# A decoder layer on one core: the combining of the gate/up products moves from VectorE to GpSimd, and the gate/up weights come packed

## The reference

```python
h = rmsnorm(x, ffn_norm[l])
gate = jnp.einsum('bsd,df->bsf', h, w_gate[l])      # d = 2048, f = 5632
up = jnp.einsum('bsd,df->bsf', h, w_up[l])
x = x + jnp.einsum('bsf,fd->bsd', jax.nn.silu(gate) * up, w_down[l])
return rmsnorm(x, final_norm)
```

## Time and profile before

| | |
|---|---|
| median of three runs | 2033.67 us |
| the profiled execution: its time, and the span of its instructions | 2032.2 us, 2030.4 us |
| ScalarE busy | 1005.3 us (50%) |
| GpSimd busy | 142.7 us (7%) |
| gate/up stage | from about 656 us (first L1524) to about 1563 us |
| granted TensorE clock, mean | 0.999 |

### The profile page before, as it was taken

The page is one execution under the profiler, slowest core; times in us unless marked ns, Lnnn a source line. Parts: engine busy times, 40 slices in busy tenths (PEclk is TensorE's granted clock), DMA queues, the critical chain, the costliest instruction groups (busy, mean ns, idle before and its releaser), DMA issues.

```text
span 2030.4 us, 30889 instructions
## 1 busy us (share of the span) xinstructions
PE 2013.3 (99%) x10492; PEld 1720.2 (85%) x10492; DVE 1528.3 (75%) x2250; ACT 1005.3 (50%) x1874; POOL 142.7 (7%) x235
## 2 busy tenths in 40 slices
PE   9999999999999999999999999999999999999998
PEld 7888888887888988888888888888888888888886
DVE  5666666666766999898999999999998546546446
ACT  6455555554436654555555455554555323333333
POOL 0122222221100000000000000000000000000000
PEclk9999999999999999999999999999999999999999
DMA  8222222224234344444444444444447653544433
GB/s 295 83 75 72 77 72 73 73 72 153 76 99 155 116 139 131 132 138 125 139 137 132 138 137 136 127 141 133 131 138 243 241 179 99 177 154 120 140 96 133
DMA packets 263774, 265.32 MB, mean 131 GB/s; under 512 B 14080, under 2 KB 194560, under 8 KB 262656
## 3 DMA queue, kind: packets, MB, share of 16 engines
q1 hardware_dynamic: 249136, 224.97, 36.8%
q0 software_dynamic: 6336, 23.07, 2.9%
q10 hardware_dynamic: 8208, 15.98, 2.2%
HBM read 232.51 MB, written 31.46 MB: 130 GB/s over the span
## 4 chain that ended last, share of the span: by engine, by line
PE 75%; DVE 10%; issue 7%; ACT 4%; DMA 3%; SPq 1%; ACTq 0%; DVEq 0%; POOLq 0%; POOL 0%
PE bank L556 20%; PE bank L560 10%; PE bank L489 10%; PE bank L490 10%; PE bank L491 10%; PE bank L445 4%; PE bank L447 4%; PE bank L446 4%; DVE t_lo L1533 3%; DMA t_raw<-in_w_up 2%; ACT probs L848 1%; ACT w_hi L805 1%; PE bank L608 1%; DVE part L1542 1%; DVE w_lo L1250 1%
## 5 line engine op out<-in xcount | busy, mean ns | idle before, releaser
L556 PE MATMUL bank<-s_two,t_hi 128*128 128x512 f32 x2352 | 609.9, 392 | 2.7 <-ACT part L1070 1.3
L1250 DVE TENSOR_TENSOR w_lo<-raw,w_hi 128x512 fp32r<-128x512 f32 x364 | 253.2, 697 | 382.0 <-ACT w_hi L805 379.9
L1030 ACT ACTIVATE t_hi<-t_raw 128x1792 fp32r<-128x1792 f32 x176 | 303.3, 1724 | 378.4 <-DVE t_raw L1527 233.2
L556 PEld LDWEIGHTS bank<-s_two,t_hi 128*128 128x128 f32 x2352 | 413.0, 188 | 67.2 <-issue 1.5
L805 ACT ACTIVATE w_hi<-raw 128x512 fp32r<-128x512 f32 x364 | 229.0, 631 | 481.0 <-PE bank L491 354.4
L560 PEld LDWEIGHTS bank<-s_two,t_lo 128*128 128x128 f32 x2352 | 338.2, 190 | 35.4
L1533 DVE TENSOR_TENSOR t_lo<-t_raw,t_hi 128x1792 fp32r<-128x1792 f32 x176 | 355.2, 2018 | 8.4 <-ACT t_hi L1030 8.1
L560 PE MATMUL bank<-s_two,t_lo 128*128 128x256 f32 x2352 | 347.6, 281 | 0.0
L489 PE MATMUL bank<-w_hi,down_hi 128*128 128x512 f32 x640 | 249.1, 389 | 0.4 <-DVE down_lo L1259 0.4
L490 PE MATMUL bank<-w_lo,down_hi 128*128 128x512 f32 x640 | 249.0, 389 | 0.0
L491 PE MATMUL bank<-w_hi,down_lo 128*128 128x512 f32 x640 | 249.0, 389 | 0.0
(11 more groups left out here) (170 smaller groups left out, 2504.4 us busy)
## 6 DMA issues: line engine op xcount, KB each, us to landing
raw<-in_w_down SPq DMA_DIRECT2D x176, 256.0 KB, 3.2
t_raw<-in_w_gate SPq DMA_DIRECT2D x174, 256.0 KB, 3.1
t_raw<-in_w_up SPq DMA_DIRECT2D x174, 256.0 KB, 3.4
raw<-in_w_in SPq DMA_DIRECT2D x136, 256.0 KB, 2.6
gu_s<-gu_mid SPq DMA_DIRECT2D x44, 512.0 KB, 5.3
gu_mid<-part POOLq DMA_DIRECT2D x43, 512.0 KB, 2.9
raw<-in_w_out SPq DMA_DIRECT2D x64, 256.0 KB, 3.2
x_row<-in_x ACTq DMA_DIRECT2D x4, 1024.0 KB, 12.0
```

The lines of the kernel that those rows point to most:

```text
L556: nc.tensor.matmul(bank[SEVEN_BANK[i]][:, :], t_hi[r][:, SEVEN[i][0], q, :], both, start=d == 0 and q == 0, stop=False, skip_group_check=True)
L1030: nc.scalar.activation(t_hi[r][:, :, :, :].rearrange("p a q c -> p (a q c)"), t_raw[r][:, 1:8, :, :].rearrange("p a q c -> p (a q c)"), AC ...
L1250: nc.vector.tensor_tensor(w_lo[:, s, :], raw[:, s, :], w_hi[:, s, :].bitcast(F32), ALU.subtract).then_inc(w_lo_done, 1)
```

## The change

Three things change. GpSimd executes `post`, with the same six instructions on the same data, each followed by the store of its group. `post` leaves VectorE's order, and GpSimd's order becomes `post(0)`, `store_gu(0)`, `post(1)`, `store_gu(1)`, `invert(3)`, `post(2)` and so on. And `w_gate` and `w_up` arrive as one array `w_gu` in which each load of 128 x 512 values is a contiguous block of 128 rows of 2 KB; before, each row was four pieces of 512 B from four places. The number of DMAs and their bytes stay the same. The conditions of ScalarE's copies are not changed.

```diff
-        for dst, w in ((t_raw[r][:, 0:2, :, :], w_gate2), (t_raw[r][:, 7:9, :, :], w_up2)):
-            yield (dst.rearrange("p j q c -> p (j q) c"),
-                   w[512 * d:512 * (d + 1), bass.ds(g * P, P)].rearrange("(k p) c -> p k c", p=P))
+        four = t_raw[r][:, :, :, :].rearrange("p a q c -> p (a q c)")
+        for i, at in ((0, 0), (1, 7 * HALF)):
+            yield (four[:, at:at + SEQ], w_gu[bass.ds(g, 1), d, i, :, :].rearrange("o p c -> (o p) c"))
...
-        def post(i, gj):
...
-                if first and j == 9:
-                    post(0, 0)
-                if j % 4 == 3:
-                    post(i, j // 4 - 1)
...
-                if first and s == 6:
-                    post(7, 1)
...
+        def post(g):
+
+            z = part_low if g == 1 else part
+            pool.wait_ge(bank_taken, taken_by(0, g))
+            if g > 1:
+                nc.gpsimd.tensor_tensor(part[:, :, :], part[:, :, :], part_low[:, :, :], ALU.add).then_inc(folded, 1)
+                pool.wait_ge(folded, g - 1)
+            nc.gpsimd.tensor_tensor(z[:, 1, :], z[:, 1, :], z[:, 5, :], ALU.add).then_inc(post_done, 1)
+            nc.gpsimd.tensor_tensor(z[:, 2, :], z[:, 2, :], z[:, 4, :], ALU.add).then_inc(post_done, 1)
+            pool.wait_ge(post_done, POSTS * g + 2)
+            nc.gpsimd.tensor_tensor(z[:, 1:3, :], z[:, 1:3, :], z[:, 0:4:3, :], ALU.add).then_inc(post_done, 1)
+            pool.wait_ge(post_done, POSTS * g + 3)
+            nc.gpsimd.tensor_tensor(z[:, 1:3, :], z[:, 1:3, :], z[:, 6:7, :].broadcast_to([P, 2, HALF]), ALU.add).then_inc(post_done, 1)
+            nc.gpsimd.tensor_tensor(z[:, 0:4:3, :], z[:, 0:4:3, :], z[:, 4:6, :], ALU.subtract).then_inc(post_done, 1)
...
         for g in range(TILES):
+            post(g)
             store_gu(g)
             if g == 1:
                 invert(3, slice(0, NT))
...
+    w_gu = np.stack([np.asarray(inputs[name])[0].reshape(DOUBLES, 4, P, TILES, P) for name in ("w_gate", "w_up")])
+    w_gu = w_gu.transpose(4, 1, 0, 3, 2, 5).reshape(TILES, DOUBLES, 2, P, 4 * P)
```

More of the change, by code:

```diff
@@ L97, with build @@
 HEAD = [("A", 0, 0), ("A", 1, 3), ("B", 0, 6), ("B", 1, 8)]
-def build(nc, x, x_turned, gain_cols, w_in, sinks, w_out, w_gate, w_up, w_down, final_norm, c_dist, c_lnm, c_band, c_slope, c_ident, x_mid, gu_mid, out):
+def build(nc, x, x_turned, gain_cols, w_in, sinks, w_out, w_gu, w_down, final_norm, c_dist, c_lnm, c_band, c_slope, c_ident, x_mid, gu_mid, out):
     spot = [(nc.sbuf_base + 63) // 64 * 64]
@@ L264, in build @@
     w_out2 = w_out[0]
-    w_gate2, w_up2, w_down2 = w_gate[0], w_up[0], w_down[0]
+    w_down2 = w_down[0]
     x2, out2 = x[0], out[0]
@@ L1816, in _ @@
         invert(2, slice(0, 2 * NT))
+        def post(g):
[11 more added lines that the diff above has]
+            nc.gpsimd.tensor_tensor(z[:, 0:4:3, :], z[:, 0:4:3, :], z[:, 4:6, :], ALU.subtract).then_inc(post_done, 1)
         def store_gu(g):
+            z = part_low if g == 1 else part
             pool.wait_ge(post_done, POSTS * (g + 1))
-            z = part_low if g == 1 else part
             nc.gpsimd.dma_start(gu_mid[g, :, :], z[:, 0:4, :].rearrange("p a c -> p (a c)")).then_inc(gu_stored, 16)
         for g in range(TILES):
+            post(g)
             store_gu(g)
@@ L1846, in constants @@
             "c_ident": np.eye(P, dtype=np.float32)}
-INPUTS = ["x", "sinks", "w_out", "w_gate", "w_up", "w_down", "final_norm"]
+INPUTS = ["x", "sinks", "w_out", "w_down", "final_norm"]
 def laid_out(inputs):
@@ L1856, in laid_out @@
     w_in = w_in[0].reshape(4, 4, P, IN_COLS // P, P).transpose(3, 0, 2, 1, 4).reshape(IN_COLS // P, 4, P, 4 * P)
-    return {"x_turned": np.ascontiguousarray(x[0].T), "gain_cols": np.ascontiguousarray(np.concatenate(cols, axis=1)),
+    w_gu = np.stack([np.asarray(inputs[name])[0].reshape(DOUBLES, 4, P, TILES, P) for name in ("w_gate", "w_up")])
+    w_gu = w_gu.transpose(4, 1, 0, 3, 2, 5).reshape(TILES, DOUBLES, 2, P, 4 * P)
+    return {"w_gu": np.ascontiguousarray(w_gu), "x_turned": np.ascontiguousarray(x[0].T), "gain_cols": np.ascontiguousarray(np.concatenate(cols, axis=1)),
             "w_in": np.ascontiguousarray(w_in)}
```

## The result

The changed kernel takes 2148.14 us, the median of five runs (2147.73 to 2150.08), against 2033.67 us of the kernel before in the same job (2033.21 to 2035.97, five runs). The ratio is 1.0565, with a 95% interval of 1.0553 to 1.0577: 5.6% slower, 114.5 us. The forecast was slower, 2396 us with a range of 2160 to 2465: the direction came out, the size did not, 362 us against 114.5. The time is next to the first rival's, 2171 us.

What follows compares the result with a forecast made beforehand. TensorE was taken to bound the kernel, at 19.54 us a group. A serial loop of 28.3 us adds 8.8 us 41 times, 361 us; with 3 us for the ends, 2032.2 + 361 + 3 = 2396 us, range 2160 to 2465.

Steps and rivals of the forecast that it cites:

- the first rival: Gate/up stage: GpSimd and VectorE take turns, or GpSimd keeps the turn; 22.9 us a group, 2171 us, chance 0.20.
- The bound: Gate/up stage: TensorE bounds at 19.54 us a group, VectorE close behind; relieving VectorE of 4.78 us is worth 0.
- The duration of GpSimd's additions: `post` on GpSimd: six additions take 9.3 us a group, 4.0 of it for 1792 columns; upper end 11.0.
- That the two engines exclude each other for whole instructions: Gate/up stage: a GpSimd addition and a VectorE instruction with both inputs in SBUF never run together.
- VectorE keeps the turn while its next instruction is at hand.: Doubles of the gate/up stage: GpSimd gets no turn until a gap in VectorE's work, read from the trace at 145 us.
- `post` ends only when VectorE has run out of doubles.: Each group: all 13.6 us of VectorE's doubles and 9.3 us of GpSimd's additions go one after the other.
- 5.4 us: Each group: ScalarE's last four copies, 2.2 us, and the store with hand-over, 3.2; neither additions nor doubles advance.
- The closed loop of 28.3 us: Post, store and copies of successive groups: 2.2 + 3.2 + 9.3 + 13.6 us in place of 19.54, 41 times.
- The first groups and the last post at 3 us, 0 to 10: First two groups and the last post beside the down stage: together 3 us added to the total, 0 to 10.
- The loads: Weight tiles in 2 KB rows: taken as 0, between 0 and 15 us of gain in a stage bound by VectorE.
- `invert(3)` behind `post(1)`: GpSimd's queue: `invert(3)` comes some 5 us later, with several doubles to spare; cost 0, or 5 us once.
- the clock: TensorE may drop to 1.2 GHz in waits of 7 us or so; all four doubles slow would make 2834 us.

Runs made afterwards that it cites:

- e3: Changed kernel with GpSimd memsets, which read nothing, in place of its additions and the combining left out: 2030.59 us, 0.9988 of the kernel before.
- e4: Changed kernel with the fold (1792-column addition) back on VectorE, GpSimd keeping the five small additions: 2086.57 us, 1.0265 of the kernel before.
- e5: Changed kernel with only the fold (1792-column addition) and stores on GpSimd, the other five additions on VectorE: 2083.32 us, 1.0248 of the kernel before.
- e9: Changed kernel with one more GpSimd addition, on 768 columns, at the end of each group: 2206.26 us, 1.0848 of the kernel before.
- e7: Kernel before, GpSimd scaling rows by constant 0.5 instead of column `inv_den`; trace only: four scalings 2.59 or 2.60 us, against 3.01 or 3.02.
- e8: Kernel before, with GpSimd multiplying each row by itself instead of scaling it; one execution, trace only: L1250 takes 1.31 us.
- e6: Changed kernel with GpSimd's fold cut from one instruction of 1792 columns into seven of 256: 2252.57 us, 1.1072 of the kernel before.
- e2: Kernel before with the combining moved to GpSimd, weights left in the old layout: 2171.67 us, 1.0678 of the kernel before.
- e1: Kernel before with the packed weights alone, the combining left on VectorE: 2031.72 us, 0.9994 of the kernel before.

## Why the prediction was wrong

- **The bound.** Right. TensorE was the bound, and what VectorE was relieved of, 4.78 us a group, is worth 0.12% at most (e3).
- **The duration of GpSimd's additions.** Right: 4.0 us for the fold, shortest 3.95.
- **That the two engines exclude each other for whole instructions.** Right, and the whole of the loss: with nothing read by GpSimd there is none (e3), and it goes by the length of what is read (e4, e5, e9).
- **"VectorE keeps the turn while its next instruction is at hand."** This is the step that failed. It rested on one pattern, in which GpSimd's instruction had a column of scalars to read besides the rows. Without the column GpSimd goes at the first end of a VectorE instruction (e7, e8), and so it does at 1166.60 us in the changed kernel. The one fold of 8.03 us is the only place of this stage in the changed kernel where VectorE did keep the turn over several instructions. The Trainium skill's rule that the first to issue gets the port ("SBUF — State Buffer", section "Who interferes with whom"), which the prediction set behind the row, is the one that the trace after follows, in 509 of 514 pairs.
- **"`post` ends only when VectorE has run out of doubles."** False with it. Six VectorE instructions fall into a post, not twelve: it lasts 14.8 us (1165.74 to 1180.58), and with 5.4 us the loop is at 20.2, below the 22.2 at which VectorE stands (in the group shown, where the store came late, 8.1 us lie between the end of the post before and the fold). The closed loop of 28.3 us was never reached; e6, which lengthens the post to 18.9 us, brings it out at 24.7.
- **The first rival's sum.** 13.6 + 9.3 = 22.9 us and 2171 us, measured 22.2 and 2148. Its too-large term is the 9.3: VectorE's busy time is 21.8, so GpSimd holds it for 8.2 us. About 0.2 us of each GpSimd instruction does not hold. The 0.4 us of idle time were not in the sum and go the other way. The lower end of the range, 2160, lay only 11 us under this sum; the missing overlap at the hand-overs is worth 41 x 1.1 = 45 us.
- **The first groups and the last post at 3 us, 0 to 10.** Too little: 12.9 us in the profiled execution (3.3 and 9.6), with a TensorE that waits 9.1 us at the start of the down stage for `down_lo`. VectorE has room there on average, but not in the first chunk.
- **The loads.** 0 to 15 us in a stage bound by VectorE was too little: some 24 us (e2 against the changed kernel). On TensorE's bound 0 was right (e1).
- **`invert(3)` behind `post(1)`, and the clock.** Right on the first, 0: VectorE reads that inverse at 759.88 us (L1620) without a wait. The clock stood at 0.994 to 0.996 over the span in place of 0.999; no run separates a cost of it, and TensorE is no longer the bound.

## What to carry to other kernels

An engine that is idle is not free capacity when its instructions and those of the engine that it would relieve exclude each other: count the time in which it reads as time of that engine, instruction by instruction, and compare the sum with the bound. Here 9.3 us of GpSimd against 4.8 us of VectorE turned an engine at 94% into the bound. A pattern that stands in one place of a trace and has one more operand than the case at hand is a weak ground for a rule; between a sum (22.9) and a loop (28.3) the range has to reach below the sum, by what overlaps at each hand-over.

## What the runs showed of the hardware

- A GpSimd instruction that reads SBUF and a VectorE instruction with two SBUF inputs ran one after the other, the one issued first ahead in 509 of 514 overlapping pairs: an addition of 256 columns, 0.41 us at the shortest, took up to 4.29 us behind a fold.
- GpSimd memsets of 1792 columns (1.60 us) beside L1533 left it at 2.03 us at most.
- GpSimd's scaling by a column in SBUF lost its turn once where the same scaling by a constant did not: 384 columns ended 0.37 us after L1292, and with the column only after the next VectorE instruction as well.
- Cutting one GpSimd instruction of 1792 columns into seven of 256 cost 104 us in the whole kernel, 2.5 us a group, a lower granted clock (0.93 in the stage) included.
